# Experts' weights brought in two pieces at a time

## The reference, cut to what matters

```
logits = xt @ w_router                       # 256 tokens, 8 experts
top_logits, top_idx = top_k(logits, 2)
top_w = softmax(top_logits)
h  = silu(ragged_dot(xs, w_gate)) * ragged_dot(xs, w_up)     # 1024 -> 2816
ys = ragged_dot(h, w_down) * top_w                           # 2816 -> 1024
out = segment_sum(ys, tok)
```

## Time and profile before

| | |
|---|---|
| median of 3 runs | 2516.16 us (2516.02 to 2516.46) |
| the profiled execution | 2514.8 us, its span 2513.0 us |
| PE busy | 2398.2 us, 95% |
| DVE busy | 1733.9 us, 69% |
| ACT busy | 1301.3 us, 52% |
| loads of experts' weights | 560 in all: 496 of 512 KB, 64 of 256 KB |
| stage of the experts | about 540 to 1321 us of the span |
| granted TensorE clock, mean | 0.987 |

### The profile page before, as it was taken

One profiled execution on the slowest core, in us unless ns is written; L12 is line 12 of the kernel. 1 busy time (PEld: TensorE's weight loads), 2 busy tenths in 40 slices (PEclk: granted clock), 3 DMA queues, 4 the chain that ended last, 5 costly groups with the idle time before them and its releaser, 6 DMA issues.

```text
span 2513.0 us, 31296 instructions
## 1 busy us (share of the span) xinstructions
PE 2398.2 (95%) x11476; PEld 1928.1 (77%) x11476; DVE 1733.9 (69%) x1983; ACT 1301.3 (52%) x1660; POOL 100.5 (4%) x135
## 2 busy tenths in 40 slices
PE   7999988999999999999997999989999999999997
PEld 4667875768888888888885888868877887887885
DVE  2577774679999999999986456674566453556556
ACT  2334333448877777878873343554444343444442
POOL 1001001000000000000001000000000000000001
PEclk9999998999999999999998999999999999999998
DMA  9869856539999989999985554346535553337550
GB/s 367 302 212 309 327 201 220 189 126 392 393 318 371 387 311 385 363 329 378 359 318 177 201 182 153 118 162 220 198 123 201 200 183 112 124 105 243 199 185 34
DMA packets 316382, 608.08 MB, mean 242 GB/s; under 512 B 15105, under 2 KB 154401, under 8 KB 309602
## 3 DMA queue, kind: packets, MB, share of 16 engines
q1 hardware_dynamic: 306432, 564.27, 63.4%
q0 software_dynamic: 9552, 41.13, 4.5%
q10 hardware_dynamic: 274, 1.05, 0.1%
HBM read 605.31 MB, written 1.08 MB: 241 GB/s over the span
## 4 chain that ended last, share of the span: by engine, by line
PE 83%; DVE 8%; DMA 3%; ACT 3%; issue 1%; POOL 1%; DVEq 0%; SPq 0%; ACTq 0%
PE G L960 48%; PE A L960 29%; PE TB L960 4%; DMA down<-in_ada_w 2%; PE TB L1438 1%; DVE w_lo L2925 1%; POOL small L2733 1%; DMA down<-in_moe_w_down 1%; PE TB L982 1%; DVE small L3338 1%; PE TB L1545 1%; DVE x_tok L3327 0%; ACT probs L2162 0%; DVE x_tok L3350 0%; DMA wide<-in_ffn_w_in 0%
## 5 line engine op out<-in xcount | busy, mean ns | idle before, releaser
L960 PE MATMUL G<-w_hi,u_hi 128*128 128x512 f32 x1592 | 622.3, 397 | 7.6 <-DVE w_lo L2925 3.4
L960 PE MATMUL G<-w_hi,u_lo 128*128 128x512 f32 x1592 | 612.3, 391 | 1.2 <-DVE u_lo L3253 1.2
L960 PE MATMUL G<-w_lo,u_hi 128*128 128x512 f32 x1592 | 612.5, 391 | 0.0
L2966 DVE TENSOR_TENSOR w_lo<-wide,w_hi 128x1024 fp32r<-128x1024 f32 x352 | 415.6, 1222 | 13.1 <-ACT w_hi L2230 3.5
L2230 ACT ACTIVATE w_hi<-wide 128x1024 fp32r<-128x1024 f32 x352 | 371.2, 1062 | 89.5 <-PE G L960 43.2
L960 PEld LDWEIGHTS G<-w_hi,u_hi 128*128 128x128 f32 x1592 | 299.0, 188 | 72.0 <-DVE w_lo L2925 7.0
L960 PEld LDWEIGHTS G<-w_hi,u_lo 128*128 128x128 f32 x1592 | 299.1, 188 | 67.2 <-DVE u_lo L3253 2.9
L960 PEld LDWEIGHTS G<-w_lo,u_hi 128*128 128x128 f32 x1592 | 300.1, 189 | 60.0
L960 PE MATMUL A<-w_hi,hidden_hi 128*128 128x512 f32 x772 | 301.4, 390 | 0.0
L960 PE MATMUL A<-w_hi,hidden_lo 128*128 128x512 f32 x772 | 300.7, 389 | 0.0
L960 PE MATMUL A<-w_lo,hidden_hi 128*128 128x512 f32 x772 | 300.4, 389 | 0.0
(11 more groups left out here) (442 smaller groups left out, 3178.6 us busy)
## 6 DMA issues: line engine op xcount, KB each, us to landing
down<-in_moe_w_down SPq DMA_DIRECT2D x176, 512.0 KB, 8.3
wide<-in_ffn_w_in SPq DMA_DIRECT2D x88, 1024.0 KB, 7.6
wide<-in_moe_w_gate SPq DMA_DIRECT2D x160, 512.0 KB, 8.6
wide<-in_moe_w_up SPq DMA_DIRECT2D x160, 512.0 KB, 9.0
down<-in_ffn_w_out SPq DMA_DIRECT2D x44, 1024.0 KB, 8.5
down<-in_ada_w SPq DMA_DIRECT2D x28, 1024.0 KB, 7.4
wide<-in_w_in SPq DMA_DIRECT2D x24, 1024.0 KB, 7.9
ada_row<-in_ada_w POOLq DMA_DIRECT2D x16, 1024.0 KB, 6.7
```

What stands on the lines that cost most here:

```text
L960: return nc.tensor.matmul(o, lhsT, rhs, start=start, stop=stop, skip_group_check=True)
L2966: V.tensor_tensor(w_lo[at % RING][:, :], raw_piece(n, at)[0], w_hi[at % RING][:, :].bitcast(F32), ALU.subtract).then_inc(lo_ready, 1)
```

## The change

`load_piece` becomes `load_two`. A call for the first of two neighbouring pieces of one kind (q even) loads both with one transfer of 1 MB (for "both" pieces two transfers of 512 KB, one of gate and one of up); the call for the second returns at once. The transfer waits for the release of the slot that the second piece will take, so for the later of the two. Both pieces have one semaphore, that of the first slot, and ACT waits for the same value for both. The order of the loads, the slots, the bytes and the instructions of PE, ACT, DVE and POOL stay.

```
@@ raw_piece, raw_loads
-                return down[j // 2 % 2][:, (j % 2) * 1024:(j % 2 + 1) * 1024], moe_down_full[j % DOWN_RING], j, DOWN_RING
+                return (down[j // 2 % 2][:, (j % 2) * 1024:(j % 2 + 1) * 1024],
+                        moe_down_full[(j - j % 2) % DOWN_RING], j, DOWN_RING)
...
+            j -= j % 2
             loads = [16 * (2 if PIECES[b][0] == "both" else 1) for b in same[j % ring::ring]]
@@ moe
-                    def load_piece(p, at):
+                    def load_two(p, at):
                         what, e, u, q = PIECES[at]
+                        if q % 2:
+                            return
+                        _, full, j, ring = raw_piece(n, at)
+                        dst = down[j // 2 % 2][:, :] if what == "down" else \
+                            wide[(n.w + j // 4) % RW][:, (j % 4) * 1024:(j % 4 + 2) * 1024]
-                        before = p * PAIR + (same[j - ring] if j >= ring else same[j - ring] - PAIR)
+                        before = p * PAIR + (same[j + 1 - ring] if j >= ring else same[j + 1 - ring] - PAIR)
                         sp.wait_ge(lo_ready, ...)
-                            sp.dma_start(dst, dns[2 * p + e, row:row + P, :]).then_inc(full, 16)
+                            sp.dma_start(dst.rearrange("p (f c) -> p f c", f=2),
+                                         dns[2 * p + e, row:row + 2 * P, :].rearrange("(f p) c -> p f c", p=P)) \
+                                .then_inc(full, 16)
...
-                            sp.dma_start(dst.rearrange("p (k f) -> p k f", k=2),
-                                         kview(part)[:, 2 * q:2 * q + 2, u * WCOLS:(u + 1) * WCOLS]).then_inc(full, 16)
+                            sp.dma_start(dst.rearrange("p (k f) -> p k f", k=4),
+                                         kview(part)[:, 2 * q:2 * q + 4, u * WCOLS:(u + 1) * WCOLS]).then_inc(full, 16)
```

More of the change, by code:

```diff
@@ L676, in raw_piece @@
                 j = DOWN_PIECES.index(at)
-                return down[j // 2 % 2][:, (j % 2) * 1024:(j % 2 + 1) * 1024], moe_down_full[j % DOWN_RING], j, DOWN_RING
+                return (down[j // 2 % 2][:, (j % 2) * 1024:(j % 2 + 1) * 1024],
+                        moe_down_full[(j - j % 2) % DOWN_RING], j, DOWN_RING)
             j = UP_PIECES.index(at)
-            return (wide[(n.w + j // 4) % RW][:, (j % 4) * 1024:(j % 4 + 1) * 1024], moe_full[j % WIDE_RING], j, WIDE_RING)
+            return (wide[(n.w + j // 4) % RW][:, (j % 4) * 1024:(j % 4 + 1) * 1024],
+                    moe_full[(j - j % 2) % WIDE_RING], j, WIDE_RING)
         def raw_loads(at):
@@ L880, in _ @@
                     sp.wait_ge(ada_used, ADA_ROWS * DEPTH)
-                    def load_piece(p, at):
+                    def load_two(p, at):
                         what, e, u, q = PIECES[at]
-                        dst, full, j, ring = raw_piece(n, at)
+                        if q % 2:
[3 more added lines that the diff above has]
+                            wide[(n.w + j // 4) % RW][:, (j % 4) * 1024:(j % 4 + 2) * 1024]
                         same = DOWN_PIECES if what == "down" else UP_PIECES
-                        before = p * PAIR + (same[j - ring] if j >= ring else same[j - ring] - PAIR)
+                        before = p * PAIR + (same[j + 1 - ring] if j >= ring else same[j + 1 - ring] - PAIR)
                         sp.wait_ge(lo_ready, n.lo + (before + 1 if before >= 0 else (0 if j >= 4 or what == "down" else -4)))
@@ L890, in load_piece @@
                             row = u * WCOLS + q * P
-                            sp.dma_start(dst, dns[2 * p + e, row:row + P, :]).then_inc(full, 16)
+                            sp.dma_start(dst.rearrange("p (f c) -> p f c", f=2),
+                                         dns[2 * p + e, row:row + 2 * P, :].rearrange("(f p) c -> p f c", p=P)) \
+                                .then_inc(full, 16)
                         elif what == "both":
-                            halves = dst.rearrange("p (k h f) -> p k h f", k=2, h=2)
+                            halves = dst.rearrange("p (k h f) -> p k h f", k=4, h=2)
                             for h, part in enumerate((gates, ups)):
-                                sp.dma_start(halves[:, :, h], kview(part[2 * p + e])[:, 2 * q:2 * q + 2, u * WCOLS:FF]) \
+                                sp.dma_start(halves[:, :, h], kview(part[2 * p + e])[:, 2 * q:2 * q + 4, u * WCOLS:FF]) \
                                     .then_inc(full, 16)
@@ L898, in load_piece @@
                             part = (gates if what == "gate" else ups)[2 * p + e]
-                            sp.dma_start(dst.rearrange("p (k f) -> p k f", k=2),
-                                         kview(part)[:, 2 * q:2 * q + 2, u * WCOLS:(u + 1) * WCOLS]).then_inc(full, 16)
+                            sp.dma_start(dst.rearrange("p (k f) -> p k f", k=4),
+                                         kview(part)[:, 2 * q:2 * q + 4, u * WCOLS:(u + 1) * WCOLS]).then_inc(full, 16)
                     for at in range(4):
-                        load_piece(0, at)
+                        load_two(0, at)
                     for p in range(PAIRS):
                         for at in range(4, PAIR - 2):
-                            load_piece(p, at)
+                            load_two(p, at)
                         if p < PAIRS - 1:
                             for at in range(4):
-                                load_piece(p + 1, at)
+                                load_two(p + 1, at)
                         for at in (PAIR - 2, PAIR - 1):
-                            load_piece(p, at)
+                            load_two(p, at)
                     for half in range(2):
```

## The result

| | before | changed |
|---|---|---|
| median of 7 runs each, in turn on one chip | 2516.16 us (2512.51 to 2518.27) | 2525.01 us (2523.01 to 2529.72) |
| profiled execution, its span | 2514.8, 2513.0 us | 2527.86, 2526.0 us |
| mean granted TensorE clock in it | 0.987 | 0.983 |

The ratio is 1.0041, interval 1.0031 to 1.0052: slower by 7.8 to 13.1 us, most likely by 10.3 us (the medians differ by 8.9). The forecast was 5.6 us.

The account below looks back on a forecast made before the run. PE was taken to set the experts' stage's pace, with one load deciding at round ends. Start 0, three inner ends of 1.3 us and last end 1.7 make 5.6; 2516.2 + 5.6 = 2521.8, say 2522 us, bounds 2517.5 to 2527.

Parts of the forecast that it names:

- the body: Inside the rounds of the experts' stage: step stays 5.44 us for four pieces, larger loads gain 0.
- The fit of 2.0 us for each load: Skill page's load cost, 2.0 us plus bytes over 436 GB/s: 3.2 us for 512 KB, 4.4 for 1 MB.
- The place: Ends of the four rounds, where the load of the last two down pieces stands in PE's chain.
- later issue and common signal: First piece of two: load issued one piece later, counted as landed only with the second; 1.3 to 3.0 us later.
- The inner ends: Three round ends with a successor: shared last down load lands 1.3 us later each, 3.9 us in all (0.3 to 6.9).
- the sum's upper bound of 10.7: Whole kernel: upper bounds of start, three inner ends and last end added; the total loss would be 1.3 to 10.7 us.
- The last end: End of the last round: ACT's first piece of the next layer starts 1.7 us later (1.0 to 2.5).
- T: Last round's end: first down piece lands at 1315.6; PE turns hidden values at T + 2.8, buffer free at T + 7.3.
- The first: Rival at round ends: landing bounded by latency, not queue; 0.1 us per inner end, 1.3 at the last; 2517.8, chance 0.17.
- The second: Rival inside the rounds: late first pieces starve PE about 1.3 us in each of eight experts; 10.4 more, 2532, chance 0.10.
- third: Rival in the experts' stage: transfers bound it, fewer loads free the queue; gain at most 5.3 us, 2511, chance 0.05.
- the fourth: Rival at round ends: no effect, copies held by something else and last end has room; 2516, chance 0.10.

Follow-up runs that it names:

- the second profile: Profile of the changed kernel, unaltered, taken when it was run once more (experiment 8): span 2516.0 us.
- Experiment 1: Changed kernel, but the last two down pieces of each round loaded and signalled one by one, as before the change: 2515.02 us, ratio 1.0003.
- Experiment 2: Kernel before, with only the last two down pieces of each round combined in one 1 MB load: 2522.91 us, ratio 1.0034.
- experiment 6: Kernel before, with the load of each round's last but one down piece issued only when the last piece's slot is free: 2513.89 us, ratio 1.0000.
- experiment 7: Kernel before, loads untouched, but ACT takes each round's last but one down piece only when the last has landed too: 2522.73 us, ratio 1.0037.
- experiment 8: Changed kernel once more, unaltered, against the kernel before on another chip: 2522.55 us, ratio 1.0030.
- experiment 10: Kernel before, with ACT rounding each round's last but one down piece in 16 parts: 2521.74 us, ratio 1.0030.
- experiment 11: experiment 10 with five more products for PE ahead of the wait at each inner round end: 2517.79 us, ratio 1.0014 to the kernel before.
- experiment 3: Kernel before, with the last two down pieces loaded ahead of the next round's first four gate pieces: 2509.97 us, ratio 0.9980.

## Why the prediction was right and wrong

**What bounds the kernel, and the body: right.** 5.44 us for four pieces as before, 395 GB/s as before, and PE loses nothing in the bodies beyond the one step of 0.4 us in the second profile. Experiment 1 shows it by the time: with the last load of each round taken out, the change is worth 1.0003. The fit of 2.0 us for each load that the working held against its rows was measured on loads issued from GpSimd (the Trainium skill, "DMA: Bandwidth & Descriptors", section "Anatomy of one DMA — SWDGE (gpsimd) path"); here SP issues them.

**The place: right.** The cost sits at the four ends and nowhere else, through the one load that the chain named. Experiment 2 makes most or all of the loss with it alone. The working gave two reasons for the delay, later issue and common signal. Experiments 6 and 7 separate them: the signal is the whole of it (1.0037), the later issue nothing (1.0000).

**The inner ends: the waits right, their price wrong.** The prediction had "PE was already waiting, so the whole 1.3 is lost. Three times: 3.9". PE's waits at the three places rose from 2.5 to 6.9 us, 4.4 more, where 3.9 was forecast (6.4 in all). In the second profile they rose by 2.6 us. The term of 3.9 lies between the two, and it held as the length of the waits. What failed is the step from a wait to a loss: it took a wait to cost its own length. In the first profile the clock fell to half behind two of the three waits, for 3.4 and 6.8 us, and that cost another 5.1 us. The prediction read "at the full granted clock" as a property of the stage, and it was one of a stage in which PE, after the first 10 us, never idled longer than 0.8 us. The missing term is 5.1 us in one profiled execution, 0 in the other. Over the runs, the change cost 10.3 us by the first ratio and 7.5 by experiment 8's; less the forecast's 5.6, this leaves 2 to 5 us for it on average. Experiments 10 and 11 show such a surplus apart from the loads (4.0 us), and experiment 7 shows the falls with not one load combined. That 10.3 us still lies under the sum's upper bound of 10.7 is luck: the bound was made of longer waits at the four ends, and had no clock in it.

**Each inner end's size.** ACT's idleness was forecast as 3.7 us, and was 3.13, 3.93 and 4.82. The third load took 7.08 us from issue to landing (5.94 before, and 5.40 in the second profile). The third load followed the end at which the clock had fallen, but that isn't shown to be the cause, and two profiles speak against it: in experiment 2 the third load took 5.82 us behind a fall of 6.8 us, and in experiment 10 the second took 6.78 with no fall before it. Why the landings differ by 1 to 2 us from end to end stays open, and with it why a wait was long enough for a fall at one end and not at another.

**The form of the wait: wrong, without effect on the sum.** The wait for DVE's copy was to grow from 0.8 to 2.1 us. It stayed at 0.8, and PE waited for ACT's copy before that (0.6, 1.4, 2.3 us). The gathering needs ACT's half first and DVE's half four products later. Both copies move with the piece, so the first to be missed takes the growth, and the second keeps its distance. Before, ACT's copy had just been in time.

**The last end: right in its path, 0.5 us too high.** The 1.7 us were forecast for ACT's first piece of the next layer, which stood at 1321.17. It starts at 1332.12 in the first profile and at 1324.60 in the second (timeline of ACT):

```profile
1324.60 2.95 ACT L2229 ACTIVATE w_hi<-wide 128x1024 fp32r<-128x1024 f32 x3 [3.78 <-PE A L969]
```

Less the delays of 9.7 and 2.2 us with which this end began, that is 1.2 us in both. The 2.0 us of the turn, used above, are another event; part of them goes in ACT's shorter wait behind it (3.78 us where it was 4.59, for the next layer's load). ACT waits for PE there and not for the transfer, so the path through the pieces decided, as worked out. T, the landing of the first down piece, was taken 0.8 us too late: ACT began on the piece at 1324.56, less 9.7 of delay 1314.8, where 1315.6 was said. The steps behind it, T + 2.8 and T + 7.3, measured 2.8 and 7.6. PE's wait before the turn was 1.8 us where about 2 was said, and no transfer stands behind the turn in the chain. The chain of the changed kernel there:

```profile
1319.38 5.09 DMA down<-in_moe_w_down
...
1324.56 1.07 ACT w_hi L2239
...
1327.40 0.44 PE TB L1554 x2
1327.84 5.49 PE A L969 x24
```

**The rivals.** The first (latency, 2517.8) fits none of the waits: ACT waited 0.7 to 2.5 us longer at the inner ends, not 0.1. The second and third are excluded by experiment 1, the fourth by the ratio.

**What stays open.** When the clock falls behind a wait: the same 1.43 and 0.8 us were followed by a fall in one execution and not in another. The profiles give the price of a single fall and count how often it came; how many falls an average run has is not recorded, so the 2 to 5 us are inferred from the times.

**The fastest version** is experiment 3, 0.9980. It follows from the same chain: if one load sets PE's pace at a round's end, it should not stand behind four loads that nobody needs yet.

## What to carry to other kernels

A larger load delays the signal of its first half. Where the consumer takes halves one at a time and the queue is full anyway, that gives nothing in rate and costs a piece's time at each place where a load stands in the chain of waits, so look for these places (the last loads of a round above all), keep them small, and put them ahead of loads that can wait. And price a new wait of a matrix engine that has been busy without gaps at more than its length, as behind seven of nine waits of 1.1 to 2.3 us here: the clock that the profile shows as full may fall behind it, in some executions and not in others, so one profile isn't enough to see it.

## What the runs showed of the hardware

- The granted clock fell to 1.2 GHz for 3.4 or 6.8 us at inner round ends where PE had waited 1.3 to 2.3 us and then 0.8 us, with dense products before and after; 0.8 us alone was followed by no fall at the three inner ends of the profile before. The Trainium skill, "TensorE: Matmul & The Clock Gate", section "Part 1: The HAM clock gate (the "warmup" mystery)", lists half and full as the two states of the clock; the granted clock in these traces is at one or the other.
- 512 KB loads and 1 MB loads in a full queue moved the same 395 GB/s (stretch of 580 to 600 us in both kernels).
- Two 512 KB loads issued back to back, each with its own signal, could be used one by one: 1.0000 (experiment 6), where a wait for both cost 1.0037 (experiment 7).
- Rounding 128 x 1024 numbers on ACT in 16 parts took 2.45 us instead of 1.06: some 0.09 us for each further part.
